# Stationary weights and moving tokens in the first feed-forward layer of a two-block forward pass

## The chip, the cores and the metric

The kernel runs on one core of a Trainium2 chip, as one launch. The metric is the device time in microseconds (us): the median of three runs of the kernel before is 2271.12 us (2270.33 to 2272.8). The profile comes from one further execution, which took 2271.82 us; the span that its trace covers is 2270.5 us.

A core has a matrix engine (TensorE; PE in the profile, with its weight loads in a row of their own, PEld), a vector engine (VectorE, DVE), a scalar engine (ScalarE, ACT), GpSimd (POOL) and DMA queues, of which SyncE (SP) starts most. A matmul holds one operand in the array (the stationary one, 128 columns here) and streams the other past it (the moving one); the result lands in one of eight PSUM banks of 128 partitions by 512 fp32 values. The stationary columns become the partitions of the result, the moving columns its free axis. In this kernel each matmul carries its own weight load.

## The reference

256 tokens with 2048 channels go through a first block (pooling and stick-breaking attention, then a feed-forward layer) and a second model part (two attention mixers). The change sits in the feed-forward layer of the first block:

```
h2 = rms_norm(x, norm2_w[l]) * (1.0 + scale2[:, None]) + shift2[:, None]
f = jnp.square(jax.nn.relu(h2 @ w_ff1[l])) @ w_ff2[l]
x = x + gate2[:, None] * f
```

w_ff1 is 2048 by 8192, w_ff2 is 8192 by 2048, all in fp32.

## The kernel before

**Precision.** Each fp32 operand is split in two fp32r parts, high and low. A product is three matmuls: high by high, high by low, low by high. `mm_tile` (L610) issues them at L625, L626 and L627 for each of the two tiles of 128 tokens.

**Chunks.** Every weight matrix is cut into chunks of 512 output columns. A chunk of a feed-forward layer has KT = 16 k steps of 128 rows each, so 16 x 2 x 3 = 96 matmuls that stream 512 columns. The activations (AH, AL, BH, BL: 128 channels on the partitions, 256 tokens on the free axis) are stationary, the weights move, and the result has tokens on the partitions. It fills two banks, `pair[0]` or `pair[1]` in turn (banks 0 and 1, or 2 and 3).

**The feed-forward stage.** For i in 0 to 3, four chunks ("f1", i, n) make 2048 of the 8192 hidden columns, and four chunks ("f2", i, n) use them. So there are 16 chunks of f1 and 16 of f2. The first chunk of f1 is woven with the normalization (`norm_chunk`, L848).

**Between the layers.** At the end of an f1 chunk ScalarE takes the two banks to `fbuf` with Relu (L1400) and squares in place (L1402). The second layer wants the hidden values with channels on the partitions, so TensorE transposes them: `turn` (L813), called at k = 4 of the next chunk (L874) and at k = 8 of the first f2 chunk (L883), does eight transposes of 128 by 128 into banks 4 and 5 (L637). ScalarE copies them to BH (L1307), VectorE forms the low part in BL from the banks (L1917). The f2 chunk sums in a pair of banks, and VectorE adds that to `merged` (L2015; for i = 0 it copies, L2012).

**Feeding the weights.** SyncE loads units of four k steps into a ring (L480). For every half unit (two k steps) ScalarE makes the high part (L1163), VectorE the low part (L1676), both three halves ahead in rings of four, and TensorE frees a slot with its semaphore `used`. Each engine works through a program written out by hand, strictly in its order; there is no scheduler. `newest` in `weight_stream` (L114) says which earlier chunk held the banks that a chunk writes, and `mm_tile` waits for that one to be emptied (L616).

**Side work.** GpSimd loads slices of w_ada and VectorE multiplies and sums them (L1696); four of their last sums across partitions (`ada_sum`, L641) fall into the feed-forward stage and use bank 7.

Of the kernel before, what the change touches and what calls it, by code (L numbers as in the profile page):

```python
# [109 lines left out]
def weight_stream(t):  # L110
# [160 lines left out]
def body(nc, t, ctx, known):  # L271
# [333 lines left out]
    def tensor_program(T):  # L605
# [3 lines left out]

        def mm_tile(c, k, stat, tiles=range(NT)):  # L610
# [20 lines left out]

        def transposes(b, src, c0):
# [8 lines left out]
        def ada_sum(c, k):  # L641
# [4 lines left out]
            if emptied[3] is not None:  # L646
                T.wait_ge(*emptied[3])
            if p in ROWS:
                mm = T.matmul(bank(3), ones[:, :], ada_acc[p % 2][:, :], start=True, stop=True)
            else:  # L650
                for j in range(AC // P):
                    mm = T.matmul(bank(3)[:, j:j + 1], ada_acc[p % 2][:, j * P:(j + 1) * P], ones[:, 0:1], start=True, stop=True)
            mm.then_inc(*done("ada_summed", p))
            emptied[3] = of("ada_kept", p)
# [193 lines left out]
        def norm_chunk(c, stat):  # L848
            norm_turn(0)
            norm_turn(1)  # L850
            for k in range(KT):
# [4 lines left out]
                mm_tile(c, k, stat)  # L856
# [9 lines left out]
        for i in range(4):  # L866
            for n in range(4):
                if i == 0 and n == 0:
                    norm_chunk(C["f1", 0, 0], STAT["f1"])
# [283 lines left out]
    def scalar_program(A):  # L1153
# [155 lines left out]
        for n in range(4):  # L1309
# [70 lines left out]
        for i in range(4):  # L1380
            for n in range(4):
                c = C["f1", i, n]
                for k in range(KT):
# [10 lines left out]
                if i == 0 and n == 0:  # L1394
                    A.wait_ge(*of("norm_turned", ("ff", 5)))
                elif i == 0 and n == 1:
# [1038 lines left out]
```

## Time and profile before

| | us |
|---|---|
| median of three runs | 2271.12 |
| lowest, highest | 2270.33, 2272.8 |
| the profiled execution | 2271.82 |
| its span in the trace | 2270.5 |
| PE busy in the span | 2206.2 |
| PEld busy | 1803.4 |
| DVE busy | 1463.9 |
| ACT busy | 1078.8 |

Busy time of PE counts a matmul from its start to its modelled end, and neighbours overlap; how long a matmul holds the engine is read from the distance between two starts. Times in the rows count from the start of the span. The first f1 chunk begins near 691 us, the last f2 chunk ends near 1413 us.

### The profile page before, as it was taken

How to read it: one execution, taken by the hardware profiler on the slowest of the kernel's cores; microseconds unless marked ns; L12 is line 12 of the kernel's file. 1: busy time of each engine (PE TensorE's matmuls, PEld its weight loads, DVE VectorE, ACT ScalarE, POOL GpSimd, SP SyncE). 2: the span in 40 equal slices, each digit the busy share in tenths (PEclk: the TensorE clock that was granted, in tenths of full speed). 3: DMA queues.
4: the chain of work that ended last, by engine and by line, in shares of the span. 5: the costliest groups of instructions: out<-in, count | busy, mean ns of one | idle time of the engine just before them, and what ended most of it. 6: DMA issues, size and time to landing. Idle time of an engine off the chain costs nothing.

```text
span 2270.5 us, 27331 instructions
## 1 busy us (share of the span) xinstructions
PE 2206.2 (97%) x10659; PEld 1803.4 (79%) x10659; DVE 1463.9 (64%) x1919; ACT 1078.8 (48%) x1599; POOL 175.9 (8%) x318
## 2 busy tenths in 40 slices
PE   6889999999998999999999999999999999999998
PEld 5777788888887888888888888877778877877777
DVE  6767878888875566565554456566665536666664
ACT  3234356544446534444443544555555524565544
POOL 0004311122210000000000000000000000000000
PEclk8889999999998999999999999999999989999999
DMA  9997866788885677777555555544445633333333
GB/s 344 331 305 271 302 206 230 252 307 304 305 288 164 228 238 238 229 237 226 185 185 192 179 193 178 186 149 149 149 154 185 215 123 126 107 112 113 110 130 130
DMA packets 242165, 468.53 MB, mean 206 GB/s; under 512 B 14363, under 2 KB 52469, under 8 KB 241397
## 3 DMA queue, kind: packets, MB, share of 16 engines
q1 hardware_dynamic: 213552, 387.74, 51.9%
q0 software_dynamic: 20480, 67.13, 8.7%
q10 hardware_dynamic: 8004, 11.93, 1.5%
q8 instruction: 85, 1.39, 0.2%
q14 instruction: 44, 0.35, 0.0%
HBM read 464.65 MB, written 2.10 MB: 206 GB/s over the span
## 4 chain that ended last, share of the span: by engine, by line
PE 88%; DVE 5%; issue 2%; ACT 2%; DMA 2%; POOL 1%; SPq 0%; ACTq 0%; DVEq 0%
PE banks L625 26%; PE banks L627 25%; PE banks L626 25%; PE banks L637 2%; PE banks L913 2%; PE banks L925 1%; DVE ada_acc_vec L1735 1%; DMA ada_w<-in_w_ada 1%; ACT w_high L1163 1%; DVE w_low L1676 1%; PE banks L940 1%; PE banks L939 1%; PE banks L1028 1%; PE banks L938 1%; DVE ada_acc L1696 1%
## 5 line engine op out<-in xcount | busy, mean ns | idle before, releaser
L1676 DVE TENSOR_TENSOR w_low<-raw,w_high 128x1024 fp32r<-128x1024 f32 x674 | 821.9, 1224 | 625.7 <-ACT w_high L1163 625.2
L1163 ACT CAST w_high<-raw 128x1024 fp32r<-128x1024 f32 x674 | 701.4, 1046 | 791.4 <-PE banks L627 791.1
L625 PE MATMUL banks<-w_high,act_a_high 128*128 128x512 f32 (+1 forms) x1696 | 691.2, 408 | 21.7 <-DVE act_a_low L1768 14.2
L626 PE MATMUL banks<-w_low,act_a_high 128*128 128x512 f32 (+1 forms) x1696 | 668.3, 394 | 0.0
L627 PE MATMUL banks<-w_high,act_a_low 128*128 128x512 f32 (+1 forms) x1696 | 668.1, 394 | 0.0
L625 PEld LDWEIGHTS banks<-w_high,act_a_high 128*128 128x128 f32 x1696 | 326.6, 193 | 103.9 <-issue 21.6
L627 PEld LDWEIGHTS banks<-w_high,act_a_low 128*128 128x128 f32 x1696 | 326.3, 192 | 69.5
L626 PEld LDWEIGHTS banks<-w_low,act_a_high 128*128 128x128 f32 x1696 | 326.6, 193 | 63.1 <-issue 2.4
L625 PE MATMUL banks<-w_high,act_b_high 128*128 128x512 f32 x640 | 250.7, 392 | 0.0
L627 PE MATMUL banks<-w_high,act_b_low 128*128 128x512 f32 x640 | 249.1, 389 | 0.0
L626 PE MATMUL banks<-w_low,act_b_high 128*128 128x512 f32 x640 | 249.0, 389 | 0.0
L509 POOL DMA_DIRECT2D ada_w<-in_w_ada x256 | 139.7, 546 | 709.6 <-DVE ada_acc L1696 614.2
L1696 DVE SCALAR_TENSOR_TENSOR ada_acc<-ada_w,cT,ada_acc 128x512 f32<-128x512 f32 x240 | 179.4, 747 | 15.6 <-DMA ada_w<-in_w_ada 12.5
L626 PEld LDWEIGHTS banks<-w_low,act_b_high 128*128 128x128 f32 x640 | 120.2, 188 | 25.1 <-issue 0.5
L627 PEld LDWEIGHTS banks<-w_high,act_b_low 128*128 128x128 f32 x640 | 120.1, 188 | 25.1
L625 PEld LDWEIGHTS banks<-w_high,act_b_high 128*128 128x128 f32 x640 | 120.2, 188 | 25.0 <-issue 0.5
L1471 ACT ACTIVATE scores<-scores,minus_max 128x128 f32<-128x128 f32 x192 | 85.0, 448 | 8.2 <-DVE minus_max L2099 6.7
L1482 ACT COPY ada_w<-banks 128x768 f32<-128x768 f32 x48 | 38.4, 800 | 94.2 <-PE banks L925 94.2
L1735 DVE SCALAR_TENSOR_TENSOR ada_acc_vec<-ada_first,cT,ada_acc_vec 128x512 f32<-128x512 f32 x88 | 66.0, 750 | 4.1 <-DMA ada_first<-in_w_ada 1.8
L625 PE MATMUL banks<-w_high,act_d_high 128*128 128x512 f32 x128 | 51.4, 401 | 1.6 <-DVE act_d_low L1917 1.6
L625 PE MATMUL banks<-w_high,act_c_high 128*128 128x512 f32 x128 | 50.9, 398 | 0.0
L627 PE MATMUL banks<-w_high,act_d_low 128*128 128x512 f32 x128 | 50.0, 391 | 0.0
(338 smaller groups left out, 2013.5 us busy)
## 6 DMA issues: line engine op xcount, KB each, us to landing
raw<-in_w_ff SPq DMA_DIRECT2D x128, 1024.0 KB, 5.2
raw<-in_w_in SPq DMA_DIRECT2D x64, 1024.0 KB, 7.0
ada_w<-in_w_ada POOLq DMA_DIRECT2D x256, 256.0 KB, 4.8
raw<-in_b_w_in SPq DMA_DIRECT2D x44, 1024.0 KB, 5.1
raw<-in_a_w_in SPq DMA_DIRECT2D x36, 1024.0 KB, 5.1
ada_first<-in_w_ada SPq DMA_DIRECT2D x64, 512.0 KB, 9.0
raw<-in_w_o SPq DMA_DIRECT2D x16, 1024.0 KB, 7.1
raw<-in_a_w_out SPq DMA_DIRECT2D x16, 1024.0 KB, 5.2
```

Source lines behind the costliest of these rows:

```text
L509: G.dma_start(ada_w[:, u % ADA_RING, :], t["w_ada"][0, q * P:(q + 1) * P, col:col + AC]).then_inc(*landed(f"ada_landed{u % ADA_RING}", u))
L625: T.matmul(out, xh, wh, start=(c.first and k == 0), stop=False)
L626: T.matmul(out, xh, wl, start=False, stop=False)
L627: last = T.matmul(out, xl, wh, start=False, stop=(c.last and k == c.nk - 1))
L637: tr = T.transpose(bank(b)[:, j * SEQ + tt * P:j * SEQ + (tt + 1) * P], src[:, tt, c0 + j * P:c0 + (j + 1) * P], ident[:, :])
L913: mm = T.matmul(bank(e)[:, c0:c0 + n], qG[o:o + HD, i % 4, tt * P:(tt + 1) * P], k_[o:o + HD, 0:n], start=True, stop=True)
L1163: A.copy(WH[:, h % SPL, :, :], split_ap(h)).then_inc(*done("high", h))
L1471: A.activation(sc[:, s, c0:c0 + n], sc[:, s, c0:c0 + n], ACT.Exp, scale=R, bias=nm[:, i // 4, j, tt:tt + 1], accum_out=sm[:, i // 4, j, tt ...
L1482: A.copy(pt[:, 2 * (i % 2):2 * (i % 2) + 2, :], banks[:, 5:7, 0:3 * P]).then_inc(*done("pt_made", (name, g, i)))
L1676: V.tensor_tensor(WL[:, h % SPL, :, :], split_ap(h), WH[:, h % SPL, :, :].bitcast(F32), ALU.subtract).then_inc(*done("low", h))
L1696: V.scalar_tensor_tensor(out=acc_, in0=w, scalar=c_, in1=acc_, op0=ALU.mult, op1=ALU.add).then_inc(*done("ada_acc", u))
L1735: V.scalar_tensor_tensor(out=acc_, in0=w, scalar=c_, in1=acc_, op0=ALU.mult, op1=ALU.add).then_inc(*done("first_vec", (i, u, kk)))
```

## The change

f1 is computed the other way round. The weights are stationary, 128 of a chunk's 512 columns at a time, and the 256 tokens move. The result has its output columns on the partitions, which is the layout that f2 wants, so the transposes of f1 go. A chunk is now 16 x 4 x 3 = 192 matmuls that stream 256 columns, where it was 96 that stream 512. Each of the four groups of 128 columns takes half of a bank, so a chunk takes four banks: 0 to 3 for even n, 4 to 7 for odd n. Relu and square stay; ScalarE then copies from `fbuf` to BH, one instruction of 128x1024 at k = 2 of the next chunk, and VectorE makes BL from `fbuf` and BH, one instruction at k = 4. The waits for banks change with that: `hidden_tile` of an even chunk waits for the chunk that last held banks 2 and 3 as well, `newest` is kept in step, and an `ada_sum` inside an odd chunk goes to bank 0.

```diff
         for n in range(4):
+            before = newest[0], newest[1]
             add(("f1", i, n), t["w_ff1"][0], 0, D * i + CH * n, KT, n % 2)
+            newest[0] = newest[1] = chunks["f1", i, n]
+            if n % 2 == 1:
+                newest[0], newest[1] = before
...
+    def hidden_banks(n):
+
+        return banks[:, 4 * (n % 2):4 * (n % 2) + 4, :]
+
+    def sum_bank(c):
+
+        return banks[:, 0, :] if c.name[0] == "f1" and c.name[2] % 2 == 1 else bank(3)
+
+    def by_columns(ap):
+
+        return ap.rearrange("p a (b n) -> p (a b) n", n=SEQ)
...
+        def hidden_tile(i, n, k):
+
+            c = C["f1", i, n]
+            h, kk = c.halves[k // c.per], k % c.per
+            if kk == 0:
+                T.wait_ge(*of("low", h))
+            if k == 0 and n % 2 == 0:
+                for last_ in ([C["f1", i, 0]] if n else [C["f2", i - 1, 2], C["f2", i - 1, 3]] if i else WO[-2:]):
+                    T.wait_ge(*freed(last_))
+                if summed_low[0] is not None:
+                    T.wait_ge(*summed_low[0])
+            if k == 0 and n % 2 == 1:
+                for b in range(4):
+                    T.wait_ge(*emptied[b])
+                    emptied[b] = freed(c)
+            out = hidden_banks(n)
+            for j in range(CH // P):
+                wh, wl = (w[:, h % SPL, kk, j * P:(j + 1) * P] for w in (WH, WL))
+                T.matmul(out[:, j, 0:SEQ], wh, AH[:, k, :], start=(k == 0), stop=False)
+                T.matmul(out[:, j, 0:SEQ], wl, AH[:, k, :], start=False, stop=False)
+                last = T.matmul(out[:, j, 0:SEQ], wh, AL[:, k, :], start=False, stop=(k == KT - 1))
+            if kk == c.per - 1:
+                last.then_inc(*done("used", h))
...
                 for k in range(KT):
-                    if k == 4 and n > 0:
-                        T.wait_ge(*of("squared", (i, n - 1)))
-                        turn("ff", (i, n - 1), fbuf[:, (n - 1) % 2, :, :])
                     ada_sum(C["f1", i, n], k)
-                    mm_tile(C["f1", i, n], k, STAT["f1"])
+                    hidden_tile(i, n, k)
             for n in range(4):
                 for k in range(KT):
                     if n == 0 and k == 0:
-                        T.wait_ge(*of("turn_low", ("ff", (i, 2), 1)))
-                    if n == 0 and k == 8:
-                        T.wait_ge(*of("squared", (i, 3)))
-                        turn("ff", (i, 3), fbuf[:, 1, :, :])
+                        T.wait_ge(*of("hidden_low", (i, 2)))
                     if n == 0 and k == 12:
-                        T.wait_ge(*of("turn_low", ("ff", (i, 3), 1)))
+                        T.wait_ge(*of("hidden_low", (i, 3)))
...
+        def hidden_high(i, n):
+            A.wait_ge(*of("squared", (i, n)))
+            A.copy(BH[:, 4 * n:4 * n + 4, :], by_columns(fbuf[:, n % 2, :, :])).then_inc(*done("hidden_high", (i, n)))
...
-                    if k == 4 and n > 0:
-                        turn_high("ff", (i, n - 1), BH, 4 * (n - 1))
+                    if k == 2 and n > 0:
+                        hidden_high(i, n - 1)
...
-                A.activation(fbuf[:, b, :, :], pair[b], ACT.Relu).then_inc(*done("pair_free", c.name))
+                A.activation(by_columns(fbuf[:, b, :, :]), hidden_banks(n)[:, :, 0:SEQ], ACT.Relu).then_inc(*done("pair_free", c.name))
...
+        def hidden_low(i, n):
+            V.wait_ge(*of("hidden_high", (i, n)))
+            ks = slice(4 * n, 4 * n + 4)
+            V.tensor_tensor(BL[:, ks, :], by_columns(fbuf[:, n % 2, :, :]), BH[:, ks, :].bitcast(F32),
+                            ALU.subtract).then_inc(*done("hidden_low", (i, n)))
...
                     if k == 4 and n > 0:
-                        turn_low("ff", (i, n - 1), BH, BL, 4 * (n - 1))
+                        hidden_low(i, n - 1)
```

The order of the instructions shows this at two places. The first is TensorE at k = 4 of the second chunk, ("f1", 0, 1). Before, with the eight transposes of `turn` (banks<-ident,ff_buf):

```order
L626 MATMUL banks<-w_low,act_a_high 128x512
L627 MATMUL banks<-w_high,act_a_low 128x512
L637 MATMUL banks<-ident,ff_buf 128x128 [waits norm_emptied_scalar,pair_scalar]
L637 MATMUL banks<-ident,ff_buf 128x128 x3
L637 MATMUL banks<-ident,ff_buf 128x128 [waits norm_emptied_scalar]
L637 MATMUL banks<-ident,ff_buf 128x128 x3
L625 MATMUL banks<-w_high,act_a_high 128x512 [waits low_vector]
```

Of the changed kernel, k = 4 of the same chunk; in both, the moving operand is named first, the stationary one second:

```order
L669 MATMUL banks<-act_a_high,w_low 128x256
L670 MATMUL banks<-act_a_low,w_high 128x256
L668 MATMUL banks<-act_a_high,w_high 128x256 [waits low_vector]
L669 MATMUL banks<-act_a_high,w_low 128x256
L670 MATMUL banks<-act_a_low,w_high 128x256
```

The transposes are gone from the chunk, and its matmuls are twice as many with half the columns. The second place is TensorE where an f2 chunk ends and the next f1 begins, from ("f2", 0, 3) to ("f1", 1, 0). Before (the wait `pair_vector` there is for VectorE to have emptied ("f2", 0, 2), a whole chunk earlier):

```order
L625 MATMUL banks<-w_high,act_b_high 128x512
L626 MATMUL banks<-w_low,act_b_high 128x512
L627 MATMUL banks<-w_high,act_b_low 128x512
L625 MATMUL banks<-w_high,act_a_high 128x512 [waits pair_vector,low_vector]
L626 MATMUL banks<-w_low,act_a_high 128x512
```

and in the changed kernel:

```order
L643 MATMUL banks<-w_high,act_b_high 128x512
L644 MATMUL banks<-w_low,act_b_high 128x512
L645 MATMUL banks<-w_high,act_b_low 128x512
L668 MATMUL banks<-act_a_high,w_high 128x256 [waits pair_vector,low_vector]
L669 MATMUL banks<-act_a_high,w_low 128x256
```

The wait has the same name, but by the code it is now for ("f2", 0, 3) too, the chunk whose last matmul stands in the row just above it. On ScalarE the copy to BH moves from k = 4 to k = 2 of the next chunk, and for n = 3 from k = 8 to k = 2 of the first f2 chunk; on VectorE the low part for n = 3 moves from k = 8 to k = 4. All else on these two keeps its place.

## Rows read from the trace of the kernel before

**Rows 1.** The page: busy time of each engine; shares of the chain that ended last.
```profile
PE 2206.2 (97%) x10659; PEld 1803.4 (79%) x10659; DVE 1463.9 (64%) x1919; ACT 1078.8 (48%) x1599; POOL 175.9 (8%) x318
...
PE 88%; DVE 5%; issue 2%; ACT 2%; DMA 2%; POOL 1%; SPq 0%; ACTq 0%; DVEq 0%
```

**Rows 2.** Waits of PE, the largest: total us, times, longest us.
```profile
PE banks L625 <- DVE act_a_low L1768: 14.2, 7, 3.0
```

**Rows 3.** Windows: stretch, us, busy by engine (instructions), PEclk, DMA share, GB/s.
```profile
691.50:696.00 4.50, 4.50 (x12) 3.52 (x12) 2.61 (x3) 4.41 (x8) 0.00 (x0) 0.50 0.13 28
719.00:787.00 68.00, 68.00 (x314) 56.57 (x313) 40.42 (x42) 33.74 (x37) 6.38 (x12) 1.00 0.70 229
...
1833.10:1835.10 2.00, 2.00 (x20) 1.96 (x18) 1.46 (x6) 1.34 (x3) 0.00 (x0) 1.00 1.08 365
1838.00:1842.00 4.00, 4.00 (x20) 4.00 (x20) 0.00 (x0) 0.59 (x1) 0.00 (x0) 0.50 0.78 266
```

**Rows 4.** Groups by line, 719 to 787 us: the two weight splits.
```profile
L1676 DVE TENSOR_TENSOR w_low<-raw,w_high 128x1024 fp32r<-128x1024 f32 x24 | 29.1, 1225 | 28.2 <-ACT w_high L1163 28.2
L1163 ACT CAST w_high<-raw 128x1024 fp32r<-128x1024 f32 x24 | 24.8, 1046 | 29.3 <-PE banks L627 29.3
```

**Rows 5.** Timeline of DVE (start us, us, instruction): the ends of two f2 chunks.
```profile
1032.73 1.21 DVE L2015 TENSOR_TENSOR merged<-merged,banks 128x1024 f32<-128x1024 f32 x1
...
1054.49 1.22 DVE L2015 TENSOR_TENSOR merged<-merged,banks 128x1024 f32<-128x1024 f32 x1
```

**Rows 6.** Timeline of ACT: the ends of two f1 chunks with a turn between them.
```profile
740.66 1.03 ACT L1400 ACTIVATE ff_buf<-banks 128x1024 f32<-128x1024 f32 x1 [1.62 <-PE banks L627]
...
763.33 1.03 ACT L1400 ACTIVATE ff_buf<-banks 128x1024 f32<-128x1024 f32 x1 [1.62 <-PE banks L627]
```

**Rows 7.** Timeline of PE and PEld around a turn in f1.
```profile
723.26 1.03 PE L637 MATMUL banks<-ident,ff_buf 128*128 128x128 f32 x8
...
724.36 0.40 PE L626 MATMUL banks<-w_low,act_a_high 128*128 128x512 f32 x1
724.37 0.19 PEld L627 LDWEIGHTS banks<-w_high,act_a_low 128*128 128x128 f32 x1
```

**Rows 8.** Timeline of PE in the b_gates chunk, nine starts apart.
```profile
1833.52 0.27 PE L625 MATMUL banks<-w_high,act_a_high 128*128 128x96 f32 x1
...
1834.53 0.27 PE L625 MATMUL banks<-w_high,act_a_high 128*128 128x96 f32 x1
```

**Rows 9.** Timeline of PE in the first f1 chunk, three starts apart.
```profile
693.13 0.63 PE L626 MATMUL banks<-w_low,act_a_high 128*128 128x512 f32 x1
...
694.41 0.63 PE L626 MATMUL banks<-w_low,act_a_high 128*128 128x512 f32 x1
```

**Rows 10.** Timeline of PE: plain fp32 matmuls of 256 columns, two instructions each.
```profile
289.01 0.59 PE L723 MATMUL banks<-band,merged 128*128 128x256 f32 x2
289.44 0.59 PE L724 MATMUL banks<-band,merged 128*128 128x256 f32 x2
```

**Rows 11.** Timeline of PE before the normalization: a matmul with nothing behind it.
```profile
679.81 0.39 PE L627 MATMUL banks<-w_high,act_b_low 128*128 128x512 f32 x1
686.85 1.97 PE L637 MATMUL banks<-ident,ff_buf 128*128 128x128 f32 x8 [6.65 <-ACT ff_buf L1353]
```

**Rows 12.** Timeline where ("f2", 2, 3) ends: its last matmul, and its sum taken.
```profile
1232.39 0.39 PE L627 MATMUL banks<-w_high,act_b_low 128*128 128x512 f32 x1
...
1232.82 1.22 DVE L2015 TENSOR_TENSOR merged<-merged,banks 128x1024 f32<-128x1024 f32 x1 [0.36 <-PE banks L627]
```

**Rows 13.** Timeline where ("f2", 0, 3) ends: the same two instructions.
```profile
874.40 0.39 PE L627 MATMUL banks<-w_high,act_b_low 128*128 128x512 f32 x1
...
875.04 1.22 DVE L2012 COPY merged<-banks 128x1024 f32<-128x1024 f32 x1
```

**Rows 14.** The chain in order of time: TensorE starting again after VectorE.
```profile
689.76 0.70 DVE act_a_low L1768
690.51 1.11 PE banks L637 x4
```

More of the change, by code:

```diff
@@ L608, in tensor_program @@
         emptied = {b: None for b in range(4)}
+        summed_low = {0: None}
         def mm_tile(c, k, stat, tiles=range(NT)):
@@ L645, in ada_sum @@
             T.wait_ge(*of("ada_acc", KT * p + KT - 1))
-            if emptied[3] is not None:
+            low = c.name[0] == "f1" and c.name[2] % 2 == 1
+            if low:
+                T.wait_ge(*freed(C["f1", c.name[1], c.name[2] - 1]))
+            elif emptied[3] is not None:
                 T.wait_ge(*emptied[3])
             if p in ROWS:
-                mm = T.matmul(bank(3), ones[:, :], ada_acc[p % 2][:, :], start=True, stop=True)
+                mm = T.matmul(sum_bank(c), ones[:, :], ada_acc[p % 2][:, :], start=True, stop=True)
             else:
                 for j in range(AC // P):
-                    mm = T.matmul(bank(3)[:, j:j + 1], ada_acc[p % 2][:, j * P:(j + 1) * P], ones[:, 0:1], start=True, stop=True)
+                    mm = T.matmul(sum_bank(c)[:, j:j + 1], ada_acc[p % 2][:, j * P:(j + 1) * P], ones[:, 0:1],
+                                  start=True, stop=True)
             mm.then_inc(*done("ada_summed", p))
-            emptied[3] = of("ada_kept", p)
+            if low:
+                summed_low[0] = of("ada_kept", p)
+            else:
+                emptied[3] = of("ada_kept", p)
         T.wait_ge(*of("ident_made"))
@@ L846, in norm_turn, with norm_chunk @@
             emptied[b] = of("norm_emptied", ("ff", i))
-        def norm_chunk(c, stat):
+        def norm_chunk():
             norm_turn(0)
@@ L855, in norm_chunk @@
                         norm_turn(k // 2 + 2)
[L856 removed]
+                hidden_tile(0, 0, k)
         def x_turn(name, n, added):
@@ L1389, in scalar_program @@
                                 xn_scale(k // 4 + 2)
-                    if k == 4 and n > 0:
-                        turn_high("ff", (i, n - 1), BH, 4 * (n - 1))
+                    if k == 2 and n > 0:
+                        hidden_high(i, n - 1)
                 b = n % 2
                 A.wait_ge(*ready(c))
-                if i == 0 and n == 0:
-                    A.wait_ge(*of("norm_turned", ("ff", 5)))
-                elif i == 0 and n == 1:
-                    A.wait_ge(*of("norm_turned", ("ff", 7)))
-                else:
-                    A.wait_ge(*of("turned", ("ff", (i, n - 2) if n >= 2 else (i - 1, n + 2), 1)))
-                A.activation(fbuf[:, b, :, :], pair[b], ACT.Relu).then_inc(*done("pair_free", c.name))
+                if i > 0 or n > 1:
+                    A.wait_ge(*of("hidden_low", (i, n - 2) if n >= 2 else (i - 1, n + 2)))
+                A.activation(by_columns(fbuf[:, b, :, :]), hidden_banks(n)[:, :, 0:SEQ], ACT.Relu).then_inc(*done("pair_free", c.name))
                 A.wait_ge(*of("pair_free", c.name))
@@ L1406, in scalar_program @@
                     casts(c, k)
-                    if n == 0 and k == 8:
-                        turn_high("ff", (i, 3), BH, 12)
+                    if n == 0 and k == 2:
+                        hidden_high(i, 3)
                     if i == 3 and n > 0 and k == 4:
@@ L1706, in ada_keep @@
                 g = gate_b[:, AC * (p % 12):AC * (p % 12 + 1)]
-                V.tensor_tensor(g, bank(3), g, ALU.add).then_inc(*done("ada_kept", p))
+                V.tensor_tensor(g, sum_bank(c), g, ALU.add).then_inc(*done("ada_kept", p))
             else:
-                V.tensor_copy(mod2f[:, 4 * (p - 4):4 * (p - 3)], bank(3)[:, 0:AC // P]).then_inc(*done("ada_kept", p))
+                V.tensor_copy(mod2f[:, 4 * (p - 4):4 * (p - 3)], sum_bank(c)[:, 0:AC // P]).then_inc(*done("ada_kept", p))
         def mean(n, size, eps, name, i):
@@ L2003, in vector_program @@
                     ada_keep(c, k)
-                    if n == 0 and k == 8:
-                        turn_low("ff", (i, 3), BH, BL, 12)
+                    if n == 0 and k == 4:
+                        hidden_low(i, 3)
                     if i == 3 and n > 0 and k == 6:
```

2 lines of the change are left out of this document (1 added, 1 removed).

## The prediction

> **What bounds the kernel.** I read the page first: TensorE is busy 97% of the span, and 88% of the chain that ended last is TensorE [rows 1]. Then the waits: the largest of TensorE's, for the low part of the normalized activations, is 14.2 us in all [rows 2]. In the windows over f1, 719 to 787 us, TensorE is busy 68.00 of 68.00 us at full granted clock (1.00, the 2.4 GHz level), with VectorE at 40.42 and ScalarE at 33.74 us [rows 3]. In that stretch ScalarE's weight splits waited 29.3 us for TensorE to free a slot, and VectorE's 28.2 us for ScalarE [rows 4]. Both feeders wait in the end for TensorE. So f1 goes at TensorE's issue pace, and what counts is the distance between matmul starts and how many there are. The 0.39 us of a matmul overlaps the next and is no pace.
>
> **The pace before.** Two sums taken after f2 chunks, with one plain chunk of 96 matmuls between, are 1054.49 - 1032.73 = 21.76 us apart [rows 5]: 226.7 ns a matmul of 512 columns. Two f1 chunks with a turn between are 763.33 - 740.66 = 22.67 us apart [rows 6], so a turn costs 0.91 us.
>
> **What is removed.** 16 turns: three in each i for n = 0 to 2, one in the first f2 chunk. 16 x 0.91 = 14.5 us, all of it on TensorE's path. The matmul that follows is ready, since its weights are three halves ahead.
>
> **What is replaced.** 1536 matmuls of 512 columns become 3072 of 256, each with its own load of 128 stationary columns; the streamed columns are the same in number. Some 11 of the 1536 run at granted clock 0.50 (1.2 GHz) up to about 696 us [rows 3], 3 starts in 694.41 - 693.13 = 1.28 us, 427 ns each [rows 9], which is 512 columns at 1.2 GHz and nothing more. There 22 halves at 213 ns cost the same. It leaves 1525 x 226.7 = 345.7 us against 3050 x p.
>
> The trace has no split-precision matmul of 256 columns, so p has to be bounded.
> - From below by the load. The b_gates chunk streams 96 columns (40 ns at 2.4 GHz) against loads of 128: nine starts take 1834.53 - 1833.52 = 1.01 us, 112 ns each, at clock 1.00 [rows 3, 8]. The stream can't explain that, so a load-and-matmul pair of this form goes no faster than 112 ns. The issue of the two instructions is inside this number too.
> - From above, if loads stay hidden: 512 columns at 2.4 GHz are 213.3 ns, so each matmul pays 13.4 ns more. If that is a fixed toll of every matmul, 256 columns take 106.7 + 13.4 = 120 ns.
> - Between them: the 13.4 ns seems to go mostly by column. Plain fp32 matmuls, which take twice the time a column, start 0.43 us apart for two instructions [rows 10], 215 ns against 213.3, so their toll is about 2 ns. At 1.2 GHz there is none [rows 9]. The load of the next matmul isn't its cause, for the last matmul before a pause of 7 us, with no load behind it, shows the same 0.39 us [rows 11]. What shows up only where a column is streamed every 0.42 ns looks like a limit of the stream's rate: 11.4 ns on 512 columns, 5.7 on 256. Then p = 106.7 + 2 + 5.7 = 114.4 ns. I take this value.
> - That the load is not hidden would give about 112 + 114 = 226 ns. The trace speaks against it: the load for the next matmul starts at 724.37, with the matmul of 724.36 [rows 7], and the pace at 512 columns has no room for 112 ns of load after 213 ns of stream.
>
> With p = 114.4 the f1 matmuls take 348.9 us, 3.2 us more than before. With 112: 341.6, 4.1 less. With 120: 366.0, 20.3 more.
>
> The Trainium skill (TensorE: Matmul & The Clock Gate, "Back-to-back issue gap") gives N / 2.4 + 2.5 ns for a warm matmul, 109 ns at 256 columns; by it alone f1 would take 332.5 us, an estimate, 13.2 less. The trace is 11 ns above this rule at 512 columns, and b_gates stands above it at fewer columns [rows 8], so the measurement decides.
>
> **What is added: a wait for the sum of the last f2 chunk.** ("f1", i, 0) now needs four banks, two of which the f2 chunk just finished still holds. TensorE stands until VectorE has emptied them, at i = 1, 2 and 3; at i = 0 the normalization is waited for anyway. For i = 3 the last matmul starts at 1232.39 and the sum at 1232.82, ending at 1234.04 [rows 12]. TensorE starts again about 0.05 us after VectorE ends (690.46 to 690.51) [rows 14], and the first matmul after a stop has its load exposed, about 0.1 us. The next matmul would have started 0.23 us after the last, at 1232.62, so 1.57 us are lost. For i = 1 VectorE gets to it 0.64 us after the last start instead of 0.43 [rows 13]; I take this for i = 2 as well, for both have side work on VectorE. Together 1.8 + 1.8 + 1.6 = 5.2 us. Behind TensorE's wait only the casts for later halves wait, which have slack [rows 4]; below it can't go by more than VectorE's 1.22 us allows, 3 x 1.3 = 3.9, above I allow 8.
>
> **At no cost.** Relu reads four half banks instead of two full ones, the same 1024 elements a partition; ScalarE copies once 1024 instead of twice 512, VectorE the same. They are needed a chunk later (for n = 3 at k = 12 of f2, some 16 us on), and both engines have half of f1 idle [rows 3]. If that cover were gone, about 1 us a chunk would show. A half feeds TensorE for 24 x 114 ns = 2.7 us, as before, so splits and DMA (share 0.70) see the same demand. The waits of `ada_sum` and of odd chunks are for things done several us earlier. PE's queue gets twice the instructions; b_gates shows the rate is possible for a few us [rows 8], not that it holds for 22.
>
> **Sum.** -14.5 + 3.2 + 5.2 = -6.1 us on the profiled execution of 2271.82 us (span 2270.5, so the span should be about 2264.4). That execution is 0.7 us above the median of the runs, 2271.12, from which I take the same: 2265.0 us. The sum turns zero at p = 116.4 ns, +0.2% (4.5 us) at 117.9, -0.2% at 114.9. I count 0.2% as the smallest change that a measurement tells from none. The forecast lies just beyond it.
>
> **The rivals.**
> 1. The load sets the pace, p = 112: the stream is shorter than a load-bound pair [rows 8], and the rate limit is hidden under it. For it: the 112 ns is the same for any short stream. Against: with 256 columns stream and load are equally long, and the stream's own toll should show. -14.5 - 4.1 + 5.2 = -13.4: 2257.7 us.
> 2. A fixed toll of 13.4 ns for every matmul, in its changeover to new weights: p = 120. The place is every one of the 3050 starts, and the point from which it decides for slower is p = 117.9. For it: the pace at 512 columns [rows 5] can't tell a toll by matmul from one by column, and here twice as many changeovers come, with load and stream both running all the time. Against: no toll when cold, little in plain fp32 [rows 9 to 11]. -14.5 + 20.3 + 5.2 = +11.0: 2282.1 us.
> 3. Loads and streams don't overlap, or the granted clock falls. The b_gates chunk ended at clock 0.50 [rows 3], after its short streams filled 40 of 112 ns. f1 before streamed 213 of every 227 ns and stayed at 1.00 [rows 3]; after, it is 107 of 114, so I don't expect a fall. Either would double f1: 3072 x 213 ns = 654 us, some 300 us more, about 2570 us. The Trainium skill (TensorE: Matmul & The Clock Gate, "The mechanism" in Part 3) says that loads overlap matmuls in flight only when their row groups differ, which is not so here; by that rule an estimate of 107 + 109 = 216 ns would come, the same case. At 512 columns the trace disagrees [rows 7].
> 4. The change does what it says, but waits at the chunk changes (8 us instead of 5.2) and p near 116 eat it: 2270 us, no change.
>
> **Chances.** The forecast (p 113.3 to 116) 0.46, of which 0.28 lies beyond -0.2% and 0.18 within; rival 1 0.22, faster; rival 2 0.20, 0.17 slower and 0.03 within; rival 3 0.04, slower; rival 4 0.08, within. So faster 0.50, same 0.29, slower 0.21. The forecast's own range is 2261 to 2270. With rivals 1 and 2 reached, 2256 to 2283; rival 3 is left out.
>
> **What would show it.** In the profile after: starts of f1 matmuls 114 ns apart in the middle of a chunk (112 is rival 1, 120 rival 2, 213 or more rival 3, to be read with the granted clock); no transposes from `ff_buf` but the 32 of the normalization; TensorE waiting for `merged` before the first f1 chunk three times, 1.3 to 1.6 us each by that view; f1 chunks about 22.0 us apart, with no added 0.9 us. The forecast is wrong if f1's pace is off by 2 ns or more, or if TensorE waits within f1 for weights or for the low parts.

## The result: 0.43% slower, where 0.27% faster was forecast

The changed kernel takes 2281.36 us (median of six runs, 2280.36 to 2283.54), the kernel before on the same chip 2271.61 us (six runs, 2270.33 to 2273.63). The ratio is 1.0043, 95% interval 1.0033 to 1.0054: 9.8 us slower (7.5 to 12.3), where 6 us faster were forecast. Rival 2, the fixed toll at every matmul, had given 2282.1 us.

### The profile after

The page after: busy time of each engine, the chain's shares, then two of its groups (busy us, mean ns, idle before and what ended it).

```profile
PE 2211.2 (97%) x12067; PEld 1869.2 (82%) x12067; DVE 1463.5 (64%) x1903; ACT 1078.1 (47%) x1583; POOL 176.1 (8%) x318
...
PE 86%; DVE 5%; DMA 3%; issue 2%; ACT 2%; POOL 1%; SPq 0%; ACTq 0%; DVEq 0%
...
L668 PE MATMUL banks<-act_a_high,w_high 128*128 128x256 f32 x1024 | 292.0, 285 | 4.9 <-DVE merged L2064 3.2
L670 PE MATMUL banks<-act_a_low,w_high 128*128 128x256 f32 x1024 | 290.4, 284 | 0.0
```

TensorE has 1408 more matmuls than before [rows 1] (1536 more in f1, 128 transposes fewer) and is still the engine that sets the end. Its busy time is only 5.0 us up and says nothing of the 9.8, since neighbours overlap. The mean of 284 ns isn't the pace either. The pace is in the distance of the starts. PE's timeline of the changed kernel in the second f1 chunk (start us, us, instruction):

```profile
729.28 0.28 PE L668 MATMUL banks<-act_a_high,w_high 128*128 128x256 f32 x1
729.40 0.28 PE L669 MATMUL banks<-act_a_high,w_low 128*128 128x256 f32 x1
729.52 0.28 PE L670 MATMUL banks<-act_a_low,w_high 128*128 128x256 f32 x1
...
730.48 0.28 PE L669 MATMUL banks<-act_a_high,w_low 128*128 128x256 f32 x1
```

Ten starts in 730.48 - 729.28 = 1.20 us: 120 ns each, where 114.4 was forecast. The ends of whole chunks agree. ACT's timeline, the Relu of two neighbouring f1 chunks, which answers to [rows 6]:

```profile
741.72 1.02 ACT L1443 ACTIVATE ff_buf<-banks 128x1024 f32<-128x1024 f32 x1 [1.78 <-PE banks L670]
...
764.76 1.02 ACT L1443 ACTIVATE ff_buf<-banks 128x1024 f32<-128x1024 f32 x1 [1.78 <-PE banks L670]
```

23.04 us for 192 matmuls, 120.0 ns each, with no turn left in it; with its turn a chunk had taken 22.67. The plain f2 chunk is what it was, 1058.81 - 1037.05 = 21.76 us in DVE's timeline after, as in [rows 5]:

```profile
1037.05 1.21 DVE L2064 TENSOR_TENSOR merged<-merged,banks 128x1024 f32<-128x1024 f32 x1
...
1058.81 1.21 DVE L2064 TENSOR_TENSOR merged<-merged,banks 128x1024 f32<-128x1024 f32 x1
```

The windows after (stretch, us, busy by engine, PEclk, DMA share, GB/s) answer to [rows 3]:

```profile
691.50:696.00 4.50, 4.50 (x26) 4.50 (x25) 2.61 (x3) 4.44 (x9) 0.00 (x0) 0.59 0.03 8
719.00:787.00 68.00, 68.00 (x569) 68.00 (x568) 39.30 (x38) 33.28 (x33) 5.98 (x11) 1.00 0.69 222
```

The granted clock stays at 1.00 with PE and PEld both busy all of the time: loads and streams do overlap, and rival 3 is out. The wait that answers to [rows 2], and those that the list of before doesn't have (total us, times, longest us):

```profile
PE banks L643 <- DVE act_a_low L1811: 15.8, 7, 3.0
...
PE banks L668 <- DVE merged L2064: 3.2, 2, 1.7
...
PE banks L668 <- DVE merged L2061: 1.6, 1, 1.6
...
PE banks L697 <- DVE ada_acc L1739: 1.3, 1, 1.3
```

The three waits for the sum of the last f2 chunk came as foreseen, 4.8 us in all by this view. The last row, for `ada_acc`, ends at 661.7 us, ahead of the first f1 matmul. Between there and the end of f2 TensorE has no wait that the kernel before lacks but those for `merged`. At ("f1", 3, 0) the two rows that answer to [rows 12] are:

```profile
1240.62 1.22 DVE L2064 TENSOR_TENSOR merged<-merged,banks 128x1024 f32<-128x1024 f32 x1 [0.36 <-PE banks L645]
```

```profile
1242.10 0.36 PE L668 MATMUL banks<-act_a_high,w_high 128*128 128x256 f32 x1 [1.52 <-DVE merged L2064]
1242.29 0.28 PE L669 MATMUL banks<-act_a_high,w_low 128*128 128x256 f32 x1
```

DVE doesn't start sooner or later than before (0.36 us of idle in both), and TensorE goes on 1242.10 - 1241.84 = 0.26 us after DVE's end (0.14 at i = 1, 0.27 at i = 2), not 0.05. The weight splits wait slightly longer than before ([rows 4] had 28.2 and 29.3 us):

```profile
L1719 DVE TENSOR_TENSOR w_low<-raw,w_high 128x1024 fp32r<-128x1024 f32 x24 | 29.1, 1225 | 29.5 <-ACT w_high L1206 29.5
L1206 ACT CAST w_high<-raw 128x1024 fp32r<-128x1024 f32 x24 | 24.8, 1045 | 30.1 <-PE banks L670 30.1
```

**Where the time went.** The first matmul of each stage, read from PE's timelines of both, cuts the difference up (us):

| stretch | before | after | difference |
|---|---|---|---|
| start to the first f1 matmul | 691.28 | 691.67 | +0.39 |
| f1, i = 0 | 94.50 | 95.93 | +1.43 |
| f1, i = 1 | 90.61 | 93.08 | +2.47 |
| f1, i = 2 | 90.61 | 93.06 | +2.45 |
| f1, i = 3 | 89.74 | 92.22 | +2.48 |
| f2, i = 0 to 2, to the next f1 | 265.62 | 268.36 | +2.74 |
| f2, i = 3, to the matmul after it | 90.66 | 89.79 | -0.87 |
| the rest | 857.44 | 858.19 | +0.75 |

A stage of f1 at 120 ns should be 768 x 120.0 - 384 x 226.7 = +5.1 us longer, less three turns of 0.91: +2.4. Three of the four stages show that. At i = 0 the granted clock rose about 1 us sooner than before (0.93 from 695 to 696 us, where before it was 0.93 from 696 to 697 us). So f1 had 1.4 us less at 1.2 GHz, by estimate 0.7 us gained. An f2 stage loses one turn, -0.9, which the last one shows alone; the other three are 0.91 longer on the mean, so each new wait took 1.8 us. From the first f1 matmul to the matmul after the last f2 the change is +10.7 us, against +11.0 in rival 2's sum. The two spans differ by 11.8 us, more than the medians' 9.8: the profiled execution of the changed kernel was the slowest of its six, 2283.54 us.

### The profile page after: what moved, and what is told of

Read it like the earlier page. It is cut to its first block, busy times and chain, and to the rows that moved or that the text cites. A ratio compares the mean times of both kernels' runs of the same rounds, so it can differ in the third digit from the quotient of the medians.

```text
span 2282.3 us, 30107 instructions
## 1 busy us (share of the span) xinstructions
PE 2211.2 (97%) x12067; PEld 1869.2 (82%) x12067; DVE 1463.5 (64%) x1903; ACT 1078.1 (47%) x1583; POOL 176.1 (8%) x318
## 4 chain that ended last, share of the span: by engine, by line
PE 86%; DVE 5%; DMA 3%; issue 2%; ACT 2%; POOL 1%; SPq 0%; ACTq 0%; DVEq 0%
PE banks L643 20%; PE banks L645 19%; PE banks L644 19%; PE banks L668 5%; PE banks L670 5%; PE banks L669 5%; DMA ada_w<-in_w_ada 2%; PE banks L956 2%; PE banks L679 2%; PE banks L968 1%; DVE ada_acc_vec L1778 1%; ACT w_high L1206 1%; DVE w_low L1719 1%; DVE ada_acc L1739 1%; PE banks L982 1%
## 5 line engine op out<-in xcount | busy, mean ns | idle before, releaser
L643 PE MATMUL banks<-w_high,act_a_high 128*128 128x512 f32 (+1 forms) x1184 | 489.2, 413 | 23.1 <-DVE act_a_low L1811 15.8
L645 PE MATMUL banks<-w_high,act_a_low 128*128 128x512 f32 (+1 forms) x1184 | 468.4, 396 | 0.0
L644 PE MATMUL banks<-w_low,act_a_high 128*128 128x512 f32 (+1 forms) x1184 | 468.1, 395 | 0.0
L643 PEld LDWEIGHTS banks<-w_high,act_a_high 128*128 128x128 f32 x1184 | 229.9, 194 | 85.0 <-issue 20.9
L668 PE MATMUL banks<-act_a_high,w_high 128*128 128x256 f32 x1024 | 292.0, 285 | 4.9 <-DVE merged L2064 3.2
L670 PE MATMUL banks<-act_a_low,w_high 128*128 128x256 f32 x1024 | 290.4, 284 | 0.0
L669 PE MATMUL banks<-act_a_high,w_low 128*128 128x256 f32 x1024 | 290.4, 284 | 0.0
L668 PEld LDWEIGHTS banks<-act_a_high,w_high 128*128 128x128 f32 x1024 | 197.4, 193 | 6.5 <-issue 6.5
L669 PEld LDWEIGHTS banks<-act_a_high,w_low 128*128 128x128 f32 x1024 | 197.3, 193 | 0.5 <-issue 0.5
L670 PEld LDWEIGHTS banks<-act_a_low,w_high 128*128 128x128 f32 x1024 | 197.2, 193 | 0.0
```

Source lines behind the costliest of these rows:

```text
L643: T.matmul(out, xh, wh, start=(c.first and k == 0), stop=False)
L644: T.matmul(out, xh, wl, start=False, stop=False)
L645: last = T.matmul(out, xl, wh, start=False, stop=(c.last and k == c.nk - 1))
L668: T.matmul(out[:, j, 0:SEQ], wh, AH[:, k, :], start=(k == 0), stop=False)
L669: T.matmul(out[:, j, 0:SEQ], wl, AH[:, k, :], start=False, stop=False)
L670: last = T.matmul(out[:, j, 0:SEQ], wh, AL[:, k, :], start=False, stop=(k == KT - 1))
```

## The experiments

Ratios are against the kernel before on the same chip. Later ones are called by their labels: e2_wide is the one with the toll taken away, e3_banks the one without the new waits, e6_merge_banks the version with fewer matmuls and these banks, and e9_merge_banks_again its second run. In kernels that work on the changed one, the diff is against it, where nothing else is said.

### A ladder of matmuls alone

```diff
+    for i in range(48):
+        T.matmul(banks[:, 4, 0:256], wr[:, i % 4, :], xr[:, 0:256], **flags(i))
+    for i in range(48):
+        T.matmul(banks[:, 5, 0:224], wr[:, i % 4, :], xr[:, 0:224], **flags(i))
...
```

> A kernel of its own, which computes nothing of the reference (it copies x to the output) and only issues streams of 48 equal matmuls one behind the other, to read the pace of each. Split precision (fp32r) with 128 stationary columns and 512, 448, 384, 320, 256, 224, 192 and 160 moving ones; then 64 stationary columns with 512 and 256; then bf16 with 512 and 256, plain fp32 with 512 and 256, and fp32r with the same stationary tile every time. Theory A (a fixed toll of every fp32r matmul, 13.3 ns): pace = N/2.4 + 13.3: 226.7, 200, 173.3, 146.7, 120, then 112 from the load for 224 and less (224 would be 106.6). Theory B (a toll by column, the forecast's): 226.7, 198.7, 170.6, 142.5, 114.4, 112, 112, 112. Theory C (a toll that comes from the load of 128 columns running beside the stream): with 64 stationary columns the toll halves or more, 512 columns take about 220 ns and 256 about 113; under A it stays 226.7 and 120. bf16: under a toll of changeover that all types share, the same 13.3 above 213.3 and 106.7.

PE's timeline: each row is a run of up to 48 matmuls, and the distance between two rows' starts by 48 is the pace. L38 to L54 are fp32r with 128 stationary columns, L56 and L58 with 64, L62 and L64 bf16, L66 and L68 plain fp32.

```profile
24.09 9.89 PE L40 MATMUL banks<-x_round,w_round 128*128 128x448 f32 x48
33.82 8.48 PE L42 MATMUL banks<-x_round,w_round 128*128 128x384 f32 x48
42.14 7.19 PE L44 MATMUL banks<-x_round,w_round 128*128 128x320 f32 x48
49.17 5.92 PE L46 MATMUL banks<-x_round,w_round 128*128 128x256 f32 x48
54.93 5.52 PE L48 MATMUL banks<-x_round,w_round 128*128 128x224 f32 x48
60.28 5.51 PE L50 MATMUL banks<-x_round,w_round 128*128 128x192 f32 x48
65.63 5.51 PE L52 MATMUL banks<-x_round,w_round 128*128 128x160 f32 x48
70.97 11.10 PE L54 MATMUL banks<-x_round,w_round 128*128 128x512 f32 x48
...
109.53 10.31 PE L62 MATMUL banks<-x_bf,w_bf 128*128 128x512 bf16 x47
119.68 5.40 PE L64 MATMUL banks<-x_bf,w_bf 128*128 128x256 bf16 x48
124.92 20.77 PE L66 MATMUL banks<-x 128*128 128x512 f32 x48
```

256 columns: (54.93 - 49.17) / 48 = 120.0 ns. 320: 146.5. 384: 173.3. 448: 202.7. The rows of 512 columns have stops in them; four rows without one, in the third ladder below, give 226.7. Less N / 2.4 these are 13.2 to 13.3 ns at 256, 320, 384 and 512 (448 shows 16.0): the toll goes by matmul, not by column, so the line of 114.4 ns is wrong with nothing else of the kernel around it. From 224 columns down the pace stands at 5.35 / 48 = 111.5 ns, the load's, as b_gates had shown [rows 8]. bf16 runs at 215.8 and 109.2 ns, plain fp32 at 429.1 and 215.8 per instruction: tolls of 2.5 ns there. The last is what the prediction had read from [rows 10], correctly. It belongs to that type, and said nothing of fp32r.

With the same stationary tile in every matmul the paces are 227.5 (one stop left out) and 119.8, so it isn't other weights that cost. But the trace has a load for each of these matmuls too, 48 for 48. No run has fp32r matmuls without loads, so whether the toll belongs to the matmul or to its load stays open.

### The toll added to the kernel before

Columns halved and all else as before: tokens on the partitions, turns, two banks.

```diff
+                parts = (slice(0, SEQ), slice(SEQ, CH)) if c.name[0] == "f1" and 0 < k < KT - 1 else (slice(0, c.width),)
+                for cs_ in parts:
-                T.matmul(out, xh, wh, start=(c.first and k == 0), stop=False)
+                    T.matmul(out[:, cs_], xh, wh[:, cs_], start=(c.first and k == 0), stop=False)
...
```

> The kernel before, transposes and all, with each f1 matmul at k = 1 to 14 split in two of 256 moving weight columns (k = 0 and 15 stay whole): 16 chunks x 14 x 6 = 1344 matmuls more, the same stationary tokens. Theory A (a toll of 13.3 ns per fp32r matmul whatever moves): +17.9 us, 2289.5. Theory B (toll by column, 114.4 ns a half): +2.8 us, 2274. Rival (the changed kernel is slow because it is the weights that are stationary, or because the stationary tile changes each time to freshly written data): no change beyond B, 2274.

2290.47 us, ratio 1.0089 (1.0075 to 1.0103): 20.2 us for 1344 more matmuls, 15.0 ns each (12.7 to 17.4). PE's timeline:

```profile
729.79 0.28 PE L628 MATMUL banks<-w_low,act_a_high 128*128 128x256 f32 x1
...
731.00 0.28 PE L629 MATMUL banks<-w_high,act_a_low 128*128 128x256 f32 x1
```

Ten starts in 1.21 us, 121 ns: 256 columns cost the same with the weights moving as with the tokens moving.

### The toll taken from the changed kernel

```diff
-                T.matmul(out[:, j, 0:SEQ], wh, AH[:, k, :], start=(k == 0), stop=False)
+                T.matmul(out[:, tt, :], xh, wh, start=(k == 0), stop=False)
...
```

> The changed kernel with its waits, banks, copies and no transposes, but the f1 matmuls as before: 96 a chunk, 512 weight columns moving, tokens stationary. The hidden values so reach the second layer in the wrong layout (that layout change is what is left out). It isolates the pace. Theory A: 1536 fewer matmuls give back 1525 x 13.3 = 20.3 us: 2281.4 - 20.3 = 2261.1, which is before - 14.5 (turns) + 5 (waits) = 2262. If the loss lay in the waits or in the second layer, it would stay near 2281.

2260.47 us, ratio 0.9954 (0.9939 to 0.9969). Against the changed kernel's 1.0043 that is 0.0089, 20.2 us (16 to 24 by the two intervals), where the toll's sum had 20.3. The waits for `merged` are still there:

```profile
PE banks L669 <- DVE merged L2065: 3.2, 2, 1.7
```

### The new waits taken away

From i = 1 the even f1 chunks use banks 0, 1, 4, 5 and the odd ones 2, 3, 6, 7. So the first f1 chunk no longer needs the banks of the f2 chunk just ended.

```diff
-                for last_ in ([C["f1", i, 0]] if n else [C["f2", i - 1, 2], C["f2", i - 1, 3]] if i else WO[-2:]):
+                for last_ in ([C["f1", i, 0]] if n else [C["f2", i - 1, 2]] if i else WO[-2:]):
...
+            if k == 0 and i > 0 and n % 2 == 1:
+                T.wait_ge(*freed(C["f2", i - 1, 3] if n == 1 else C["f1", i, 1]))
```

> The changed kernel with other banks for i = 1 to 3: even chunks take banks 0, 1, 4, 5, odd ones 2, 3, 6, 7, so that a first f1 chunk no longer waits for the sum of the f2 chunk just finished, but for the one before. Relu becomes two instructions of half size. All theories of the pace leave it alone: the three waits of 1.6 to 1.8 us go, 2281.4 - 5 = 2276.3. If what follows the wait was late as well (weights, low parts), less comes back.

2276.49 us, ratio 1.0023 (1.0013 to 1.0033), 0.0020 or 4.5 us under the changed kernel (1.2 to 7.8 by the two intervals), with 5.2 worked out. The three f2 stages before a next f1 take 5.4 us less in its trace. PE's timeline where ("f2", 2, 3) ends:

```profile
1234.77 0.39 PE L651 MATMUL banks<-w_high,act_b_low 128*128 128x512 f32 x1
1235.00 0.28 PE L675 MATMUL banks<-act_a_high,w_high 128*128 128x256 f32 x1
```

The next start comes 0.23 us on, with no gap.

### Both taken away

Wide matmuls with these banks: what is left is the removal of the turns.

```diff
+    def hidden_bank(i, n, j):
+        return banks[:, 4 * (n % 2) + j if i == 0 else 2 * (n % 2) + 4 * (j // 2) + j % 2, :]
...
-                T.matmul(out[:, j, 0:SEQ], wh, AH[:, k, :], start=(k == 0), stop=False)
+                T.matmul(hidden_bank(i, n, tt)[:, :], xh, wh, start=(k == 0), stop=False)
```

> Both removed at once: f1 matmuls with 512 moving weight columns as before (layout wrong for the second layer, which is what is left out) and the banks that take away the wait at the first f1 chunk. What is left of the change against the kernel before is only that the turns are gone and the copies moved. Theory: 16 turns x 0.91 us = 14.5 us below before: 2270.8 - 14.5 = 2256.3. If the turns were partly hidden by something, less; 2260.5 (the run without the bank change) less 5 is 2255.5.

2255.22 us, ratio 0.9924 (0.991 to 0.9937): 17.3 us under before (14.3 to 20.4), which the 14.5 us for 16 turns lies just inside. From the first f1 matmul to the matmul after the last f2 its trace has 706.7 us, before it was 721.7: 15.0 us less. The turns were sized rightly, and the gain that the change was to bring is real; the toll took it.

### Does the toll go with the stationary columns?

```diff
+    for i in range(48):
+        T.matmul(banks[0:32, 6, 0:384], wr[:, i % 4, 0:32], xr[:, 0:384], **flags(i))
...
+    for i in range(48):
+        T.matmul(banks[:, 4, 0:512], wr[:, i % 4, :], xr[:, 0:512], **flags(i))
+        T.matmul(banks[:, 5, 0:256], wr[:, (i + 1) % 4, :], xr[:, 0:256], **flags(i))
```

> A second kernel of its own that computes nothing of the reference and only issues streams of 48 equal fp32r matmuls: stationary columns M = 128, 96, 64, 32 each with N = 512, 384, 256 moving, then 64 rows instead of 128, then matmuls of 512 and 256 columns in turn. The first such kernel gave N/2.4 + 13.3 ns for M = 128 down to N = 256, but 113.3 ns (a toll of 6.7) for M = 64, N = 256 and about 229 for M = 64, N = 512. Theory A1 (the toll is paid when new stationary columns take over, one array cycle for four columns): 13.3, 10, 6.7 and 3.3 ns for M = 128, 96, 64, 32, so at N = 256 120, 116.7, 113.3, 110 ns, and the same above 213.3 at N = 512 but for whatever made 229. Theory A2 (a constant toll, and M = 64 with N = 256 an exception): 120 everywhere at N = 256. Rows should not matter: 120 and 226.7 with 64 rows. In turn, 512 and 256 take 346.7 ns a pair under both.

384 moving columns take 173.9, 175.0, 173.3 and 173.3 ns with 128, 96, 64 and 32 stationary columns; 512 take 226.7, 230.0, 230.0 and 231.7. The toll doesn't shrink with the stationary columns. At 256 moving columns fewer stationary ones do show less (119.8, 116.0, 113.3, 117.8), in no order that I can explain. The last part brought something new. PE's timeline of 512 and 256 columns in turn:

```profile
196.21 0.28 PE L79 MATMUL banks<-x_round,w_round 128*128 128x256 f32 x1
196.33 0.40 PE L78 MATMUL banks<-x_round,w_round 128*128 128x512 f32 x1
...
199.74 0.28 PE L79 MATMUL banks<-x_round,w_round 128*128 128x256 f32 x1
```

Ten pairs in 3.53 us: 353 ns a pair, where the two paces alone add up to 346.7. Over the whole row, four pairs at a time, it is 350 to 355.

### A version with fewer tolls

If a toll is due at every matmul, there should be fewer. The high weights meet both token halves: AH and AL are put in one tensor, and one matmul streams AH and AL (512 columns) past wh, a second one AH past wl (256). Per k step 8 matmuls instead of 12. The two halves of a bank are then summed at the eviction: ScalarE copies one, VectorE adds the other and does Relu and square.

```diff
+                T.matmul(two(out[:, j, :]), wh, A2[:, :, k, :], start=(k == 0), stop=False)
+                last = T.matmul(out[:, j, SEQ:CH], wl, AH[:, k, :], start=False, stop=(k == KT - 1))
...
+                V.tensor_tensor(by_columns(f_), by_columns(f_), hidden_banks(n)[:, :, 0:SEQ], ALU.add).then_inc(*done("pair_free", c.name))
...
+                V.scalar_tensor_tensor(out=f_, in0=f_, scalar=0.0, in1=f_, op0=ALU.max, op1=ALU.mult).then_inc(*done("squared", (i, n)))
```

> The changed kernel with two matmuls instead of three for each 128 by 128 weight tile: the high weights meet the high and the low activations in one matmul of 512 moving columns (256 of each), into both halves of the bank, and the low weights add their 256. The two halves are summed when the bank is emptied (ScalarE copies one, VectorE adds the other from the bank, then makes relu squared in one instruction). 1024 + 1024 matmuls a stage quarter, 2048 in all for 3072: 1024 tolls fewer. Theory A (a toll by matmul): 1024 x 13.3 = 13.6 us less than the changed kernel, 2281.4 - 13.6 = 2267.8, minus nothing else; the waits at the first f1 chunk stay. Theory B (a toll by streamed column): no gain, 2281.

2272.37 us, ratio 1.0003 (0.9994 to 1.0012). It gets back 0.0040, 9.1 us, of the 13.6 us that 1024 tolls are. With the banks of the run above as well:

```diff
+                T.matmul(two(hidden_bank(i, n, j)), wh, A2[:, :, k, :], start=(k == 0), stop=False)
...
```

> The same with the banks of e3 as well, which took 4.9 us from the changed kernel: 2276.5 - 13.6 = 2262.9, so 0.35% faster than the kernel before and 0.8% faster than the changed one. If ScalarE and VectorE can't empty the banks in time (VectorE does 2.4 us more a chunk), TensorE would wait for weights at the chunk ends, up to a few us in all.

2268.4 us, ratio 0.9983 (0.9974 to 0.9992). The same kernel on another chip:

> The same kernel as e6_merge_banks, run beside e8 on one chip: ratio 0.9983 again, 0.9974 to 0.9992; nothing else is tested.

2268.58 us, ratio 0.9988 (0.9979 to 0.9997). So this version beats both kernels, the one before by 0.12 to 0.17%, but not by the 0.35% that was expected. PE's timeline (of the first of the two) shows why:

```profile
764.45 0.40 PE L675 MATMUL banks<-act_a,w_high 128*128 128x512 f32 x1
764.69 0.28 PE L676 MATMUL banks<-act_a,w_low 128*128 128x256 f32 x1
...
765.51 0.40 PE L675 MATMUL banks<-act_a,w_high 128*128 128x512 f32 x1
```

Three pairs in 1.06 us: 353 ns a pair again, some 6.6 ns above the sum. Not every pair takes that long: in this trace some 610 of the 1024 do, 4.2 us in all (the end of the next section has the others). That is about the miss, 0.9983 against 2262.9 / 2270.8 = 0.9965, or 4.1 us. In e5_merge some 530 do, 3.6 us, where 4.5 are missing. VectorE's and ScalarE's new work isn't behind it: PE has no wait for `ff_buf` or the banks in f1.

### Where the 6 ns of a pair come from

```diff
+    for i in range(48):
+        T.matmul(banks[:, 3, 0:512].rearrange("p (a n) -> p a n", a=2), wr[:, i % 4, :], far[:, :, i % 8, :], **flags(i))
...
```

> A third kernel of its own that computes nothing of the reference and only issues streams of 48 equal fp32r matmuls. It asks why the 512-column matmul of e5 and e6, whose moving operand is two pieces of 256 columns 16 KB apart, took 230 to 241 ns instead of 226.7: the same 512 columns in one piece (226.7), in two neighbouring pieces written as two, in two pieces 16 KB apart with other addresses each time, and in one piece with other addresses each time. If the jump costs, only the third is slower, by 4 to 12 ns. If reading other addresses each time costs, the fourth is too. And it asks where the load of 128 columns takes over: 288, 272, 256, 248, 240 columns give N/2.4 + 13.3 = 133.3, 126.7, 120, 116.6, 113.3 ns as long as that is above 112. Last, 64 and 32 stationary columns with 288, 320 and 192 moving: a constant toll gives 133.3, 146.7 and 93.3 ns.

One piece, two pieces, two pieces 16 KB apart, other addresses: four neighbouring runs, all 10.88 / 48 = 226.7 ns.

```profile
27.41 11.04 PE L43 MATMUL banks<-x_round,w_round 128*128 128x512 f32 x48
38.29 11.04 PE L45 MATMUL banks<-x_round,w_round 128*128 128x512 f32 x48
49.17 11.04 PE L47 MATMUL banks<-x_far,w_round 128*128 128x512 f32 x48
60.05 11.04 PE L49 MATMUL banks<-x_far,w_round 128*128 128x512 f32 x48
```

Between 240 and 288 columns the pace goes 112.1, 114.9 (248), 120.0 (256), 125.2 (272), 131.7 (288): the line meets the floor of 111.5 near 240, and at 248, 272 and 288 the toll is 11.6 to 11.9 ns, not 13.3. With 64 and 32 stationary columns and 192 moving the pace is 88.6 and 88.4 ns, under that floor, so the floor goes with the 128 stationary columns. In the kernel, with AH and AL side by side (diff against e6_merge_banks):

```diff
-    A2 = sb("act_a", [P, 2, KT, SEQ], 16512, F32R)
+    A2 = sb("act_a", [P, KT, 2, SEQ], 16512, F32R)
```

> e6 with the high and low activations of a k step side by side in memory, so that the moving operand of 512 columns is one piece. If the jump of 16 KB is what costs, the 1024 matmuls of 512 columns go from a mean of 236 to about 229 ns (with the cold ones in it): about 5 to 7 us less than e6, 2262 to 2264, 0.4% faster than the kernel before. If the addresses don't matter, 2268 as e6. Rival: the writes of the activations, now in pieces of 256 with gaps, or the stationary tiles of the other layers, now at other strides, get slower, and some of it is given back.

2269.93 us, ratio 0.9993 (0.9984 to 1.0002), and its stages i = 1 to 3 take 90.11, 90.11 and 90.44 us, as in e6_merge_banks. The jump between two pieces is not the cause. Then the order within a k step, four matmuls of 512 columns and then four of 256 (against e6_merge_banks too):

```diff
             for j in range(CH // P):
-                wh, wl = (w[:, h % SPL, kk, j * P:(j + 1) * P] for w in (WH, WL))
-                T.matmul(two(hidden_bank(i, n, j)), wh, A2[:, :, k, :], start=(k == 0), stop=False)
-                last = T.matmul(hidden_bank(i, n, j)[:, SEQ:CH], wl, AH[:, k, :], start=False, stop=(k == KT - 1))
+                T.matmul(two(hidden_bank(i, n, j)), WH[:, h % SPL, kk, j * P:(j + 1) * P], A2[:, :, k, :], start=(k == 0), stop=False)
+            for j in range(CH // P):
+                last = T.matmul(hidden_bank(i, n, j)[:, SEQ:CH], WL[:, h % SPL, kk, j * P:(j + 1) * P], AH[:, k, :], start=False, stop=(k == KT - 1))
```

> The kernel of e6_merge_banks with the order inside a k step changed: first the four matmuls of 512 columns, then the four of 256, so that the column count changes twice a k step and not eight times. Theory A (the 6 ns that a pair of 512 and 256 columns takes above 226.7 + 120.0 come with each change of the column count): 1024 pairs x 6.4 ns x 3/4 = 4.9 us less than e6, some 2263.5 us on a chip whose kernel before takes 2272, ratio 0.9962; starts 226.7 apart in a row of 512s and 120 in a row of 256s. Rival B (the 6 ns go with the PSUM address, or with reading both operand halves, in f1 and not with the change): no difference to e6, ratio 0.9983.

2267.93 us, ratio 0.9984 (0.9975 to 0.9993): no different from e9_merge_banks_again beside it, where 4.9 us were expected. PE's timeline:

```profile
766.81 0.63 PE L676 MATMUL banks<-act_a,w_low 128*128 128x256 f32 x4
767.28 1.09 PE L674 MATMUL banks<-act_a,w_high 128*128 128x512 f32 x4
768.21 0.64 PE L676 MATMUL banks<-act_a,w_low 128*128 128x256 f32 x4
```

The four of 512 take 0.93 us, 232 ns each, and the four of 256 take 0.47. Every plain chunk of this kernel takes 22.45 us for its 64 pairs, 350.8 ns a pair.

The alternating order has two paces, and the totals hide it. A plain chunk of e6_merge_banks, e7_merge_beside and e9_merge_banks_again takes either 22.61 us (353.3 ns a pair) or 22.19 us (346.7, the bare sum of the two paces). The last three chunks of i = 0 and all of i = 3 go at the slower. At i = 1 and 2 the stream starts at the slower and changes where the two plain fp32 instructions of `ada_sum` interrupt it, then holds the faster to the end of the stage. PE's timeline of e6_merge_banks at i = 1, the interruption and three pairs later on:

```profile
902.58 1.02 PE L700 MATMUL banks<-ada_acc,ones 128*128 128x512 f32 x2
...
940.19 0.39 PE L675 MATMUL banks<-act_a,w_high 128*128 128x512 f32 x1
...
941.23 0.39 PE L675 MATMUL banks<-act_a,w_high 128*128 128x512 f32 x1
```

Three pairs in 1.04 us. In e5_merge i = 1 goes at the faster from its start. The grouped order is 2.5 ns a pair under the slower pace and 4.1 above the faster. Over a run both come to the same, 4.2 us above the sum, which is why e8_merge_grouped and e9_merge_banks_again measure alike. So the 6.6 ns are not the price of having both sizes in one stream. What sets the pace, and why an interruption can change it, stays open: no run tells it.

## Why the prediction was wrong

- **The pace of 256 columns, the step that failed.** The prediction wrote that the 13.4 ns "seems to go mostly by column" and took p = 106.7 + 2 + 5.7 = 114.4 ns. It is 120.0. The term was +20.3 us and not +3.2; the 17.1 us between them cover the miss (9.8 + 6.1 = 15.9). Its own upper bound was the truth.
- **Three pieces of evidence led there, and each is a true reading with a wrong conclusion.** Plain fp32 does pay only 2.5 ns [rows 10], but the toll goes with fp32r. At 1.2 GHz there is none [rows 9]: the halves before 695 us start 213 ns apart after as well. The last matmul before a pause lasts 0.39 us too [rows 11]; a duration whose end is modelled isn't evidence of a pace at all, nor of what makes it. From "only where a column is streamed every 0.42 ns" it doesn't follow that the cost is by column. The argument for the other side needed only one size, and so neither could be told from [rows 5].
- **The point of decision was right.** The zero of the sum was put at 116.4 ns and slower from 117.9; 120.0 is past both, and rival 2's 2282.1 us is within 0.8 us of the median. It had a chance of 0.20.
- **The turns were right.** -14.5 us; the ledger has 0.9 us for each, and with toll and waits both gone the kernel gains 17.3 us (14.3 to 20.4), 15.0 in its trace.
- **The waits were right.** 5.2 us foreseen, 1.8 us each in the ledger, 4.5 us back with the other banks (5.4 in the trace). In detail TensorE starts again 0.14 to 0.27 us after VectorE's end; the prediction had 0.05 and 0.1 for the load.
- **The load was hidden, and the clock stayed.** Both windows at 1.00, PEld busy for 68.00 of 68.00 us. The Trainium skill (TensorE: Matmul & The Clock Gate, "The mechanism" in Part 3) says that loads overlap matmuls in flight only where the row groups differ, which would expose every load here; the same section also lets a load into the background weight buffer go ahead. 120.0 ns for a matmul of 106.7 ns beside a load that sets a floor of 111.5 ns excludes the first here. Its "Back-to-back issue gap" of N / 2.4 + 2.5 ns agrees with bf16 (215.8 and 109.2 ns) and is 10.8 ns short for fp32r at both sizes.
- **The edits put at nothing cost nearly nothing.** Relu, copy and low part hide as said. The wait of 1.3 us for `ada_acc` lies at 661.7 us, before the first f1 matmul, and not in the traces of e2_wide and e3_banks, so it isn't put down to the change.

## What to carry to other kernels

When a change keeps the streamed columns and raises the number of matmuls, price the number first: one pace at one size can't split a toll by matmul from one by column, and the conservative reading is by matmul. Evidence on a toll from another data type or another clock level doesn't carry over; a second size of the same type does, and a run of 48 matmuls alone settles it. A layout change that saves transposes can still pay, if little, when operands that share a stationary tile are streamed in one matmul, as in the version above at 2268.4 us (0.1 to 0.2%). And a total can hide two paces: before a rule is drawn from a mean, compare the chunks of one trace with each other.

## What the runs showed of the hardware

- At full granted clock an fp32r matmul with 128 stationary columns takes N / 2.4 + 13.3 ns from start to start for N = 256, 320, 384 and 512, with its load hidden (11.6 to 11.9 at 248, 272 and 288, 16.0 at 448); bf16 and plain fp32 pay about 2.5 ns an instruction.
- With fp32r the pace never went under 111.5 ns with 128 stationary columns. With 64 or 32 of them and 192 moving columns it is 88.6 and 88.4 ns.
- fp32r matmuls of 512 and 256 columns in turn take 353.3 ns a pair or 346.7, the sum of the two paces alone. A stream changed from one to the other only at an interruption. Four by four they take 350.8.
